# The attention gate moved from the residual to the output projection's weights, on GpSimd

## The chip, the core and the metric

The kernel runs on one core of one Trainium2 chip. The metric is the device time of one execution in microseconds. Several runs of the same kernel are given by their median.

## The reference

A decoder trunk of two layers on 256 tokens of 1024 channels. Each layer is a token mixer and a mixture of experts, both modulated by a condition c:

```python
def reference(x, c, ...):
    cs = jax.nn.silu(c)
    for i in range(DEPTH):                                # 2
        mod = (cs @ ada_w[i] + ada_b[i])[:, None, :]
        sh1, sc1, g1, sh2, sc2, g2 = jnp.split(mod, 6, axis=-1)
        hm = x * (1.0 + sc1) + sh1
        if i == 0:
            y = multiscale_pool_mixer(hm, ...)            # ... @ w_out
        else:
            y = dilated_attention_mixer(hm, ...)          # mixed @ w_out
        x = layer_norm(ALPHA * x + (1.0 + g1) * y, ln1_g[i], ln1_b[i])
        hf = x * (1.0 + sc2) + sh2
        y = moe_ffn(hf, ...)                              # 64 experts, top 8, one shared
        x = layer_norm(ALPHA * x + (1.0 + g2) * y, ln2_g[i], ln2_b[i])
    return x
```

The attention has 16 heads of 64 channels in three dilation groups. Its projection matrix is 1024 x 9216, its output matrix `attn_w_out` 1024 x 1024. The gate (1 + g1) of layer 1 has 1024 values, one for each output channel: it multiplies the columns of `mixed @ attn_w_out`.

## The kernel before

The program is written by hand, engine by engine, with semaphores. Each engine runs its own list in order. SyncE's queue issues the large loads, GpSimd's the small ones.

There are four residual-and-norm stages, n = 0 to 3: behind the pooling mixer, the first experts, the attention (n = 2) and the second experts. Stage n = 2 is what the change touches. `residual(n, t, b)` on VectorE handles token tile t (128 tokens) and channel half b (512): it waits until TensorE has finished that block of y in PSUM (`y_ready`), multiplies y by the gate in place (line 1007), adds ALPHA * x into `tmp` (line 1009, scalar_tensor_tensor) and takes bn_stats (line 1011). `variance` and `deviation` finish a tile's statistics with ScalarE's square root between them (line 740). ScalarE then writes the normalised x (line 745). TensorE transposes it, ScalarE and VectorE modulate it (lines 702 and 983), and TensorE begins the shared expert (`shared_up`, line 1430) and the router. The experts' loop comes behind.

The weights of the attention come in 40 slices of 128 x 2048 f32, 1 MB each: 36 of `attn_w_in` and, as slices 36 to 39, the four of `attn_w_out` (slice q holds its rows of two 128-channel blocks, 1024 columns each). A slice passes through these steps:

- SyncE issues its load into one of four places (`load_slice`, line 569). It first waits until slice n - 4 has been used up (`w_lo`).
- ScalarE rounds it to fp32r into one of three pairs of parts (`slice_high(n)`, line 839), after the landing (`raw_in`) and after TensorE is done with slice n - 3.
- VectorE subtracts, which leaves the low part (`slice_low(n)`, line 470, `w_lo`).
- TensorE multiplies with three products for each block: high by high, low by high, high by low (lines 1589 to 1591). `project(n)` does this for slices below 36, `out_project(c)` for the output matrix. Block c = 7 is the last; it needs the last head.

ScalarE copies each projection out (line 868) and takes slice n + 3 right after it. The order of the heads is written out: in head h TensorE runs the projections that `proj_of_head(h)` lists, then perhaps a sum of modulations, the scores of head h + 1 (line 1655), the transposes of head h's probabilities (line 1679), more projections, and the product with v (line 1696). Output blocks 0 and 1 run in head 11, 2 and 3 in head 12, 4 and 5 in head 13, 6 in head 14, 7 behind head 15. VectorE, head by head: the ALiBi bias (line 1239) and maximum (line 1244) of the next head, the final modulation sum (`ada_final`, line 955 for a gate), a copy of transposed probabilities (line 1267), `slice_low` for the `before` projections, the copy of the head's output (line 1278), `mixed_low` (line 1255: the low part of the mixed heads, which `out_project` needs), `slice_low` for the others, and a `gemv`.

`gemv` is the second piece that matters here. Modulation vectors 16 to 23 are made on VectorE: a slice of 2 MB of `ada_w` is multiplied and summed with eight operations of 128 x 512 (the first on line 936, the others on line 938: scalar_tensor_tensor of the weights and the running sum, both in SBUF), four of them in each of two heads. The last one of a gemv signals `ada_acc`. TensorE then sums it over the partitions (`ada_sum`, line 1327 for a gate), and SyncE's queue loads the next `ada_w` slice into the same place. Slices 16 and 17 are the gate of layer 1's mixer, slices 22 and 23 that of its experts:

```python
def gemv_of_head(h):
    return (18 + h // 2, h % 2) if h < 10 else (ADA_SLICES - 1, h % 2) if 12 <= h < 14 else None

def sum_of_head(h):
    return (17 + h // 2 if h < 10 else 22) if h % 2 and 3 <= h <= 9 or h == 10 else None
```

```python
GEMV_LOADS = (9, 13, 19, 24, 28, 33, 39)
...
    for n in range(RAW, SLICES):
        if n in GEMV_LOADS:
            m = 17 + GEMV_LOADS.index(n)
            sp.wait_ge(ada_acc, m - 10)
            load_ada(m)
        sp.wait_ge(w_lo, n - RAW + 1)
        load_slice(n)
```

So the load of `ada_w` slice 23, and behind it that of weight slice 39, wait for the end of gemv 22 (`ada_acc` 13), whose second half stands in head 9. Head 10 on TensorE has `ada_sum(22)` ahead of the scores of head 11.

GpSimd applies the norms' gains (`gain`, lines 462 and 464) while the other engines go on with the next stage, loads the small vectors, and has nothing to do from 671 us to 942 us.

Of the kernel before, what the change touches and what calls it, by code (L numbers as in the profile page):

```python
# [22 lines left out]
ALU = mybir.AluOpType  # L23
# [3 lines left out]
P = 128  # L27
D = 1024
# [14 lines left out]
BATCHES = HEADS // HB  # L43
# [14 lines left out]
ALPHA = (2 * LAYERS) ** 0.25  # L58
# [70 lines left out]
def build(nc, a, out):  # L129
    ctx = ExitStack()  # L130
    with ctx:
        def sb(name, shape, dt=F32):
            return ctx.enter_context(nc.sbuf_tensor(name, shape, dt))

        def sem(name):
            return ctx.enter_context(nc.semaphore(name))
# [6 lines left out]
        x = sb("x", [P, TT, D])  # L143
        gate = sb("gates", [P, 2, D])
# [47 lines left out]
        def phase(name, byte, shape, dt=F32):  # L192

            return nc.alloc_sbuf_tensor_at(name, shape, dt, offset=arena + 4 * UNITS * UNIT + byte)
# [18 lines left out]
        tmp = phase("residual_or_h", 0, [P, TT, D])  # L213
# [30 lines left out]
        def units(u0, n):  # L244
            return W[:, u0 * UNIT:(u0 + n) * UNIT]
# [52 lines left out]
        RAW = 4  # L298
        RAW_UNITS = (9, 10, 5, 8)
        SLICES = 9 * BATCHES + 4  # L300

        def slice_w(n):
            return units(RAW_UNITS[n % RAW], 1).rearrange("p (k n) -> p k n", k=KD)
# [6 lines left out]
        sum_mm, sum_read, gate_in = sem("ada_sum_mm"), sem("ada_sum_read"), [sem(f"gate_bias_in{i}") for i in range(2)]  # L310
# [10 lines left out]
        y_read = sem("y_read")  # L321
# [8 lines left out]
        shw_in = sem("shared_in")  # L330
        raw_in = [sem(f"slice_in{n}") for n in range(RAW)]
        w_hi, w_lo = sem("slice_high"), sem("slice_low")
        dist_in = sem("dist_in")
        proj_mm, proj_copied = sem("proj_mm"), sem("proj_copied")
        s_mm, s_biased, max_ready, p_exp, t_mm = sem("s_mm"), sem("s_biased"), sem("max_ready"), sem("p_exp"), sem("p_T_mm")
# [67 lines left out]
        def mixer_bank(n, t):  # L403

            return ((4, 0), (0, 2), (6, 4), (0, 2))[n][t]
# [46 lines left out]
        def gain(engine, ops, step, n, tiles=range(TT)):  # L452

            engine.wait_ge(lnp_in, 32 * (n + 1))
            if n < 3:
                engine.wait_ge(hT_mm, 4 * n + 8)
            if n in (0, 2):
                engine.wait_ge(hi_ready, TT * (n // 2 + 1))
                engine.wait_ge(lo_ready, TT * (n // 2 + 1))
            for t in tiles:  # L460
                engine.wait_ge(norm_ready, TT * n + t + 1)
                step(ops.tensor_tensor(x[:, t], x[:, t], lnp[:, 0], ALU.mult))
                step.settle()
                ops.tensor_tensor(x[:, t], x[:, t], lnp[:, 1], ALU.add).then_inc(x_ready[t], 1)
            for t in tiles:
                engine.wait_ge(x_ready[t], n + 1)
# [145 lines left out]
        def _(pool):  # L612
            step = Steps(pool, pool_steps)
            G = nc.gpsimd
            def load_norm(n):
                L, s = n // 2, n % 2
                for i, name in enumerate((f"ln{s + 1}_g", f"ln{s + 1}_b")):
                    pool.dma_start(lnp[:, i, :], a[name][L][None, :].broadcast_to([P, D])).then_inc(lnp_in, 16)

            def load_router(L):  # L620
                pool.dma_start(rw[:, :, :], a["router_w"][L].rearrange("(p k) e -> p k e", k=KD)).then_inc(rw_in, 16)
# [50 lines left out]
            pool.wait_ge(proj_copied, 1)  # L672
            gain(pool, G, step, 1)
            load_norm(2)
            pool.wait_ge(o_ready, HEADS)
            load_router(1)
            first_values(1)
# [8 lines left out]
        def _(act):  # L686
# [146 lines left out]

            def slice_high(n):
                if n < SLICES:
                    act.wait_ge(raw_in[n % RAW], 16 * (n // RAW + 1))
                    if n >= 3:
                        act.wait_ge(proj_mm, n - 2)
                    copy(wr[n % 3][:, 0], slice_w(n)).then_inc(w_hi, 1)  # L839

            load_sqrt()
            ada_copy(12)
            slice_high(0)
            ada_copy(13)
            norm(1, (0,))
# [5 lines left out]
            for t in range(TT):  # L851
# [7 lines left out]
                for half in range(2):  # L859
                    ks = slice(4 * half, 4 * half + 4)  # L860
                    copy(tokens_in(hThi, ks, t), tokens_out(t, ks)).then_inc(hT_act, 1)
            slice_high(1)
            slice_high(2)

            def projected(n):
# [52 lines left out]
        def _(dve):  # L918
            step = Steps(dve, dve_steps)
            V = nc.vector  # L920
# [80 lines left out]
            def residual(n, t, b):  # L1001

                y = PS[:, mixer_bank(n, t) + b, :]
                c = slice(b * HALF, (b + 1) * HALF)
                count = 2 * TT * n + 2 * t + b + 1
                dve.wait_ge(y_ready, count)
                V.tensor_tensor(y, y, gate[:, n % 2, c], ALU.mult).then_inc(y_read, 1)
                dve.wait_ge(y_read, count)
                step(V.scalar_tensor_tensor(tmp[:, t, c], x[:, t, c], ALPHA, y, ALU.mult, ALU.add))
                step.settle()  # L1010
                step(V.bn_stats(stats[:, t, b], tmp[:, t, c]))

# [754 lines left out]
```

## Time and profile before

| | us |
|---|---|
| median of 3 runs | 1489.09 (1487.87 to 1489.23) |
| the profiled execution | 1488.59 |
| its span | 1486.4 |
| busy: TensorE | 1425.0 (96%) |
| busy: VectorE | 577.5 (39%) |
| busy: ScalarE | 407.9 (27%) |
| busy: GpSimd | 57.7 (4%) |

The span has these stages: the pooling layer and its router to about 185 us, the first experts' loop to 630, the attention from 630 to 943, norm, shared expert and router of layer 1 to 991, the second experts' loop to the last norm at about 1475. The TensorE weight load overlaps its matmuls. A line of the timeline gives start, duration, engine, source line, operation, tiles, and in brackets how long the engine sat idle before it and who ended that. Where several instructions are merged, the duration is that of the group and xN the count. A line of busy time by stretch gives the stretch and its length in us, then busy us and (x instructions) of TensorE's matmuls, its weight loads, VectorE, ScalarE and GpSimd, the granted clock, the DMA engines' mean busy share and GB/s. The granted clock is that of TensorE as a share of 2.4 GHz: 1.00 or 0.50.

### The profile page before, as it was taken

The page shows a single profiled execution, that of the slowest core. Times are in us where ns is not written, and L with a number is a line of the kernel's source. Part 1 is how long each engine was busy: PE and PEld are TensorE (multiplying, and loading weights), DVE is VectorE, ACT ScalarE, POOL GpSimd, SP SyncE. Part 2 cuts the span into 40 slices and gives each one's busy share as a digit, 9 for nine tenths or more (in the row PEclk, how much of TensorE's full clock was granted, in tenths as well). Part 3 has the DMA queues.
Part 4 walks back from the last instruction along what each step waited for, and adds up shares of the span by engine and source line. Part 5 has one row for each costly group of instructions (what it writes and reads, how often), then busy time and mean ns, then how long its engine had stood idle before and what let it go on. Part 6 is the DMA issues. An engine that isn't in the chain of part 4 may idle for free.

```text
span 1486.4 us, 19346 instructions
## 1 busy us (share of the span) xinstructions
PE 1425.0 (96%) x7546; PEld 809.1 (54%) x7546; DVE 577.5 (39%) x1109; ACT 407.9 (27%) x636; POOL 57.7 (4%) x44
## 2 busy tenths in 40 slices
PE   6999999999999999989999999699999999999994
PEld 3544444444444444479999998454444444444442
DVE  0575122222222222377767668642222222222225
ACT  1223121212121212254555445421111111212122
POOL 0001300000000000030000000002000000000001
PEclk9999999999999999989999999899999999999997
DMA  9995899999999999968356451659999999999990
GB/s 391 423 427 216 328 413 426 426 427 424 429 424 428 424 428 425 425 263 340 118 195 251 183 203 45 255 213 416 426 427 425 428 425 427 425 427 426 425 397 28
DMA packets 50511, 522.16 MB, mean 351 GB/s; under 512 B 5632, under 2 KB 5888, under 8 KB 8224
## 3 DMA queue, kind: packets, MB, share of 16 engines
q1 hardware_dynamic: 48512, 514.61, 83.3%
q0 software_dynamic: 1952, 6.88, 1.3%
q8 instruction: 34, 0.56, 0.1%
q14 instruction: 13, 0.11, 0.0%
HBM read 520.42 MB, written 1.05 MB: 351 GB/s over the span
## 4 chain that ended last, share of the span: by engine, by line
PE 89%; DVE 4%; DMA 4%; ACT 2%; issue 1%; SPq 0%; DVEq 0%; ACTq 0%
PE psum L1538 30%; PE psum L1563 15%; PE psum L1490 9%; PE psum L1499 9%; PE psum L1589 5%; PE psum L1590 5%; PE psum L1591 5%; DMA weights<-in_ada_w 3%; PE psum L1430 2%; PE psum L1358 2%; DMA weights<-in_sh_w_down 1%; PE psum L1550 1%; PE psum L1696 1%; PE psum L1455 1%; PE psum L1679 1%; PE psum L1403 1%
## 5 line engine op out<-in xcount | busy, mean ns | idle before, releaser
L1538 PE MATMUL psum<-weights,slots_of_tokens 128*64 128x512 f32 x2048 | 450.4, 592 | 0.0
L1538 PEld LDWEIGHTS psum<-weights,slots_of_tokens 128*64 128x64 f32 x2048 | 146.9, 137 | 292.7 <-issue 292.7
L1563 PE MATMUL psum<-weights,hidden_T 128*64 128x512 f32 x1024 | 233.8, 598 | 0.0
L1192 DVE SCALAR_TENSOR_TENSOR slot_rows<-psum,slot_weight,slot_rows 128x512 fp32r<-128x512 f32 x128 | 96.1, 751 | 193.9 <-ACT slot_rows L829 193.9
L1178 DVE TENSOR_TENSOR hidden<-gate,psum 128x256 f32<-128x256 f32 x64 | 27.0, 421 | 368.3 <-ACT gate L821 368.3
L1490 PE MATMUL psum<-slot_matrix,h_parts 128*128 128x512 f32 x576 | 157.3, 399 | 0.0
L1499 PE MATMUL psum<-slot_rows,slots_T 128*128 128x512 f32 x528 | 139.3, 406 | 3.7 <-DVE slot_rows L1192 3.7
L1563 PEld LDWEIGHTS psum<-weights,hidden_T 128*64 128x64 f32 x1024 | 67.8, 136 | 132.8 <-issue 132.8
L821 ACT ACTIVATE gate<-psum 128x256 f32<-128x256 f32 x64 | 24.6, 384 | 404.6 <-PE psum L1538 404.6
L1499 PEld LDWEIGHTS psum<-slot_rows,slots_T 128*128 128x128 f32 x528 | 94.0, 188 | 74.6 <-issue 57.3
L829 ACT ACTIVATE slot_rows<-psum,slot_weight 128x512 fp32r<-128x512 f32 x128 | 88.0, 687 | 136.3 <-PE psum L1563 136.3
L1589 PE MATMUL psum<-h_transposed_high,slice_parts 128*128 128x256 f32 x384 | 111.1, 289 | 6.2 <-DVE h_transposed_low L1222 6.2
L1490 PEld LDWEIGHTS psum<-slot_matrix,h_parts 128*128 128x128 f32 x576 | 103.6, 189 | 19.2 <-issue 1.0
L1590 PE MATMUL psum<-h_transposed_low,slice_parts 128*128 128x256 f32 x384 | 109.6, 286 | 0.0
L1591 PE MATMUL psum<-h_transposed_high,slice_parts 128*128 128x256 f32 x384 | 109.5, 285 | 0.0
L470 DVE TENSOR_TENSOR slice_parts<-weights,slice_parts 128x2048 fp32r<-128x2048 f32 x40 | 91.3, 2298 | 24.3 <-ACT slice_parts L839 24.3
L1180 DVE CAST slots_T<-psum 128x256 fp32r<-128x256 f32 x64 | 27.2, 425 | 161.2 <-PE psum L1552 161.2
L1589 PEld LDWEIGHTS psum<-h_transposed_high,slice_parts 128*128 128x128 f32 x384 | 74.7, 194 | 8.0 <-issue 7.6
L823 ACT COPY hidden_T<-psum 128x256 f32<-128x256 f32 x64 | 23.8, 373 | 190.2 <-PE psum L1552 190.2
L839 ACT CAST slice_parts<-weights 128x2048 fp32r<-128x2048 f32 x40 | 75.7, 1895 | 0.0
L1590 PEld LDWEIGHTS psum<-h_transposed_low,slice_parts 128*128 128x128 f32 x384 | 74.8, 195 | 0.0
L1591 PEld LDWEIGHTS psum<-h_transposed_high,slice_parts 128*128 128x128 f32 x384 | 74.7, 195 | 0.0
(187 smaller groups left out, 1421.2 us busy)
## 6 DMA issues: line engine op xcount, KB each, us to landing
weights<-in_exp_w_gu SPq DMA_DIRECT2D x128, 2048.0 KB, 14.4
weights<-in_exp_w_down SPq DMA_DIRECT2D x128, 1024.0 KB, 13.9
weights<-in_attn_w_in SPq DMA_DIRECT2D x36, 1024.0 KB, 5.4
weights<-in_ada_w SPq DMA_DIRECT2D x12, 2048.0 KB, 19.5
slots_of_tokens<-in_ada_w SPq DMA_DIRECT2D x11, 2048.0 KB, 8.6
weights<-in_pool_w_in SPq DMA_DIRECT2D x2, 2048.0 KB, 25.9
weights<-in_pool_w_out SPq DMA_DIRECT2D x2, 2048.0 KB, 23.3
weights<-in_sh_w_gu SPq DMA_DIRECT2D x2, 2048.0 KB, 10.4
```

Source lines behind the costliest of these rows:

```text
L470: ops.tensor_tensor(wr[n % 3][:, 1], slice_w(n), wr[n % 3][:, 0].bitcast(F32), ALU.subtract).then_inc(w_lo, 1)
L829: nc.scalar.activation(yw[:, 0, half * HALF:(half + 1) * HALF], PS[:, BD + half, :], ACT.Copy, scale=wslot[:, 0:1]).then_inc(lo.yh, 1)
L839: copy(wr[n % 3][:, 0], slice_w(n)).then_inc(w_hi, 1)
L1192: V.scalar_tensor_tensor(yw[:, 1, c], PS[:, BD + half, :], wslot[:, 0:1], yw[:, 0, c].bitcast(F32), ALU.mult, ALU.subtract).then_inc(lo.yl, 1)
L1358: last = mm(PS[:, u_bank(half, t), :], hT[:, k, t * P:(t + 1) * P], w_in[part][:, k - 4 * part, half * HALF:(half + 1) * HALF], start=k == ...
L1490: last = mm(PS[:, bank, :], hfs[:, s, t, k, :], Pm[b][:, t, :], start=s == 0 and t == 0, stop=s == 1 and t == TT - 1)
L1499: last = mm(PS[:, 2 * t + half, :], PT[:, t * P:(t + 1) * P], yw[:, s, half * HALF:(half + 1) * HALF], start=False, stop=True, skip_group_ ...
L1538: last = mm(PS[j * SLOTS:(j + 1) * SLOTS, BGU, :], XgT[ob][:, k, s0:s0 + SLOTS], gu_w(ws + j)[:, k, :], start=k == 0, stop=k == KD - 1, ti ...
L1563: last = mm(PS[j * SLOTS:(j + 1) * SLOTS, BD + half, :], HT[:, k, j * SLOTS:(j + 1) * SLOTS], dn_w(ws + j)[:, k, half * HALF:(half + 1) * ...
L1589: mm(out, *parts(0, 0), start=first, stop=False)
L1590: mm(out, *parts(1, 0), start=False, stop=False)
L1591: return mm(out, *parts(0, 1), start=False, stop=last)
```

## The change

For the attention's norm the gate no longer multiplies y. GpSimd multiplies the four slices of the output matrix by the gate in place, after their landing and before ScalarE rounds them. ScalarE waits for GpSimd (`w_gated`) where it waited for the landing. `residual` leaves the product out for n = 2; for the others it stays, and `y_read` is signalled by the scalar_tensor_tensor in place of the product.

```diff
@@ semaphores
+        w_gated = sem("slice_gated")
@@ GpSimd
             gain(pool, G, step, 1)
             load_norm(2)
+            pool.wait_ge(sum_read, 18)
+            for n in range(9 * BATCHES, SLICES):
+                pool.wait_ge(raw_in[n % RAW], 16 * (n // RAW + 1))
+                rows = slice_w(n).rearrange("p k n -> p (k n)").rearrange("p (k n) -> p k n", k=2)
+                G.tensor_tensor(rows, rows, gate[:, 0:1, :].broadcast_to([P, 2, D]), ALU.mult).then_inc(w_gated, 1)
             pool.wait_ge(o_ready, HEADS)
             load_router(1)
@@ ScalarE, slice_high(n)
-                    act.wait_ge(raw_in[n % RAW], 16 * (n // RAW + 1))
+                    if n < 9 * BATCHES:
+                        act.wait_ge(raw_in[n % RAW], 16 * (n // RAW + 1))
+                    else:
+                        act.wait_ge(w_gated, n - 9 * BATCHES + 1)
@@ VectorE, residual(n, t, b)
                 dve.wait_ge(y_ready, count)
-                V.tensor_tensor(y, y, gate[:, n % 2, c], ALU.mult).then_inc(y_read, 1)
+                if n != 2:
+                    step(V.tensor_tensor(y, y, gate[:, n % 2, c], ALU.mult))
+                    step.settle()
+                V.scalar_tensor_tensor(tmp[:, t, c], x[:, t, c], ALPHA, y, ALU.mult, ALU.add).then_inc(y_read, 1)
                 dve.wait_ge(y_read, count)
-                step(V.scalar_tensor_tensor(tmp[:, t, c], x[:, t, c], ALPHA, y, ALU.mult, ALU.add))
                 step.settle()
                 step(V.bn_stats(stats[:, t, b], tmp[:, t, c]))
```

## Rows read from the trace of the kernel before

**Rows 1.** Busy time by stretch, 100 us of the second experts' loop.
```profile
1100.00:1200.00 100.00, 100.00 (x462) 46.05 (x460) 26.12 (x53) 20.36 (x35) 0.00 (x0) 1.00 1.01 426
```

**Rows 2.** Timeline, VectorE, the attention's norm: start us, duration us, instruction.
```profile
943.65 0.70 DVE L1007 TENSOR_TENSOR psum<-psum,gates 128x512 f32<-128x512 f32 x1 [1.62 <-PE psum L1591]
944.39 0.69 DVE L1009 SCALAR_TENSOR_TENSOR residual_or_h<-x,psum 128x512 f32<-128x512 f32 x1
...
952.93 0.15 DVE L1018 TENSOR_SCALAR mean_variance<-mean_variance 128x1 f32<-128x1 f32 x1
```

**Rows 3.** Timeline, TensorE, last output product and first matmul of the shared expert.
```profile
946.35 0.40 PE L1591 MATMUL psum<-slice_parts,h_transposed_high 128*128 128x512 f32 x1
...
955.47 5.70 PE L1430 MATMUL psum<-weights,h_transposed 128*128 128x512 f32 x8 [1.58 <-ACT h_transposed L702]
```

**Rows 4.** Shared down weights: issue on SyncE's queue; DMA view, us to landing last.
```profile
942.48 0.43 SPq L511 DMA_DIRECT2D weights<-in_sh_w_down  x1
...
weights<-in_sh_w_down SPq DMA_DIRECT2D x1, 1024.0 KB, 10.3
```

**Rows 5.** Timeline, GpSimd: two products in other stages, then two beside the VectorE operations of rows 8.
```profile
129.71 0.73 POOL L648 TENSOR_TENSOR shared_hidden<-shared_hidden,shared_gate 128x256 f32<-128x256 f32 x1 [7.23 <-ACT shared_gate L764]
...
175.49 2.37 POOL L464 TENSOR_TENSOR x<-x,norm_gain_bias 128x1024 f32<-128x1024 f32 x1
...
658.75 4.34 POOL L464 TENSOR_TENSOR x<-x,norm_gain_bias 128x1024 f32<-128x1024 f32 x1
663.05 2.59 POOL L462 TENSOR_TENSOR x<-x,norm_gain_bias 128x1024 f32<-128x1024 f32 x1
```

**Rows 6.** Slices 37, 38, 39: issue, then the DMA view of that issue, us to landing.
```profile
878.44 0.33 SPq L569 DMA_DIRECT2D weights<-in_attn_w_out  x1
...
weights<-in_attn_w_out SPq DMA_DIRECT2D x1, 1024.0 KB, 4.8
...
880.65 0.33 SPq L569 DMA_DIRECT2D weights<-in_attn_w_out  x1
...
weights<-in_attn_w_out SPq DMA_DIRECT2D x1, 1024.0 KB, 5.7
...
887.10 0.43 SPq L569 DMA_DIRECT2D weights<-in_attn_w_out  x1
...
weights<-in_attn_w_out SPq DMA_DIRECT2D x1, 1024.0 KB, 10.0
```

**Rows 7.** Timeline, ScalarE: it rounds slice 37.
```profile
892.19 1.89 ACT L839 CAST slice_parts<-weights 128x2048 fp32r<-128x2048 f32 x1
```

**Rows 8.** Timeline, VectorE, beside the last two of rows 5.
```profile
660.75 2.62 DVE L936 TENSOR_SCALAR modulation_sums<-slots_of_tokens,condition_silu 128x512 f32<-128x512 f32 x1
663.41 2.77 DVE L938 SCALAR_TENSOR_TENSOR modulation_sums<-slots_of_tokens,condition_silu,modulation_sums 128x512 f32<-128x512 f32 x1
```

**Rows 9.** Timeline of head 9 and 10: VectorE's subtraction and second half of gemv 22, TensorE's sum.
```profile
881.38 2.29 DVE L470 TENSOR_TENSOR slice_parts<-weights,slice_parts 128x2048 fp32r<-128x2048 f32 x1 [0.46 <-ACT slice_parts L839]
883.59 3.11 DVE L938 SCALAR_TENSOR_TENSOR modulation_sums<-slots_of_tokens,condition_silu,modulation_sums 128x512 f32<-128x512 f32 x4
...
891.50 1.02 PE L1327 MATMUL psum<-modulation_sums,constants 128*128 128x512 f32 x2
```

**Rows 10.** Timeline, VectorE, head 10: slices 36 and 37, then the mixed heads.
```profile
897.70 4.47 DVE L470 TENSOR_TENSOR slice_parts<-weights,slice_parts 128x2048 fp32r<-128x2048 f32 x2
...
902.31 1.28 DVE L1255 TENSOR_TENSOR h_transposed_low<-mixed_heads_T,h_transposed_high 128x512 fp32r<-128x512 f32 x2
```

**Rows 11.** Timeline, TensorE, head 11; output blocks 0 and 1 between the two.
```profile
902.73 1.06 PE L1679 MATMUL psum<-constants,scores 128*128 128x128 f32 x8 [0.26 <-DVE mixed_heads_T L1278]
...
909.68 1.09 PE L1696 MATMUL psum<-probabilities_T,qkv 128*64 128x128 f32 x16 [0.42 <-DVE probabilities_T L1267]
```

**Rows 12.** Busy time by stretch, columns as in rows 1; the clock is third from the end.
```profile
40.00:80.00 40.00, 38.02 (x123) 23.11 (x122) 25.03 (x38) 11.05 (x22) 0.00 (x0) 0.96 1.01 425
...
42.00:44.00 2.00, 0.22 (x2) 0.13 (x2) 1.53 (x5) 1.51 (x4) 0.00 (x0) 1.00 1.09 455
```

## The prediction, made before the change had run

> **What bounds the kernel now.** I first asked what the later half of the span is paced by. In the expert loop TensorE is busy for the whole of each stretch while the DMA engines also run near their top rate [rows 1]. So a microsecond gained or lost before that loop moves the end by a microsecond, and nothing in the loop gives it back. The change touches two places ahead of the loop: the residual and norm behind attention (943 to 955 us), and the last four weight slices (862 to 920 us). I read the first on VectorE's and TensorE's timelines, then who waits for whom in the second.
>
> **What the change removes.** Behind attention VectorE runs, four times over, a product by the gate in PSUM (line 1007), a scalar_tensor_tensor (1009) and bn_stats (1011). The first product starts at 943.65 and the next step at 944.39, so one product is 0.74 us on VectorE's queue [rows 2]. TensorE has issued its last product at 946.35 (done 946.75) [rows 3]. With the products gone VectorE would run 943.65, 945.0, 946.8 (after the 0.4 us of variance) and 948.4 for its four blocks. TensorE's results are there before each of these, so no wait takes the products' place: the variance that ended at 952.93 + 0.15 [rows 2] would end at about 950.2. Four times 0.72 is 2.9 us gained on that variance. What TensorE waits for at 955.47 [rows 3] is ScalarE's modulated columns. They stand behind the first tile's norm, which only three of the products hold up (3 x 0.72 = 2.2 us), and behind the second tile's root, which all four do. So they come 2.2 to 2.9 us earlier. There is a second floor. The shared expert's weights also have to be there: issued at 942.48, landed 10.3 us later, at 952.8 [rows 4]. That caps the gain at 955.47 - 952.8 = 2.7. The gain is 2.2 to 2.7 us; I take 2.4.
>
> The other three norms keep their products. Their y_read now comes one instruction (0.7 us) later. Only GpSimd's gate loads wait for it, hundreds of microseconds before those gates are used: cost nothing.
>
> **What it adds.** GpSimd multiplies slices 36 to 39 (128 x 2048 f32, both inputs in SBUF) in place. Its tensor_tensor takes 0.73 us on 256 columns and 2.37 on 1024 [rows 5], so 2.135 ns a column, and 2.37 + 1024 x 0.002135 = 4.56 us for 2048. The bounds are 4.5 and 4.8 (twice 2.37 and a bit), since the row is straight and the forms differ only in the gate read twice. The Trainium skill (GPSIMD Engine Reference, section 3.1) gives 4497 ns for a two-input f32 operation of this size; by an estimate from it, the sum would be 0.2 us lower over three of them.
>
> ScalarE now waits for the gated slice, not for the landing. Slice 37 is issued at 878.44 and lands 4.8 later at 883.24; slice 38 at 880.65, landing 5.7 later at 886.35 [rows 6]. ScalarE wants slice 37 at 892.19 [rows 7], slices 38 and 39 later. Each gated slice is ready before, even with GpSimd held up as below (888.2 and 893.5). Slice 36 lands at about 867 and meets VectorE idle. GpSimd has nothing queued behind these waits but the router load, which waits for the last head anyway. So the new wait itself costs nothing, and it costs at once if a gating slips by over 4 us.
>
> **The cost that decides: GpSimd and VectorE hold each other up.** The trace of before has one stretch where both work on SBUF. GpSimd's 1024-column product at 658.75 took 4.34 instead of 2.37 while VectorE ran a subtraction. Then VectorE's tensor_scalar at 660.75 took 2.62, and its scalar_tensor_tensor at 663.41 took 2.77 [rows 5, 8], where four of the same form take 3.11 with nothing beside them, 0.78 each [rows 9]. The ends fit a strict alternation: GpSimd's first product ends at 663.09, VectorE's at 663.37, GpSimd's next at 665.64, VectorE's next at 666.18. Whoever waits goes in when the other's instruction ends, and holds the other for its whole length. By this rule each of the new operations can hold VectorE for 4.56 us.
>
> [...]
>
> First collision. GpSimd asks for slice 37 at 883.3, while VectorE subtracts (881.38 + 2.29 = 883.67). It is let in at 883.67 and holds until 888.23. VectorE's four modulation products, 3.11 us together from 883.59 [rows 9], then get one turn (to 888.98). GpSimd, with slice 38 long there, takes 888.98 to 893.54. The other three products end at 893.54 + 3 x 0.78 = 895.9, where before they ended at 886.7. TensorE needs their sum: ada_sum(22) ran at 891.50 with no wait [rows 9]. It now waits until 895.9: **+4.4 us** on TensorE, the scores of head 11 and all behind them.
>
> Second collision. The end of the same products releases SyncE's last modulation load and slice 39. Its issue at 887.10 goes to 896.3, and it landed 10.0 us after issue [rows 6], so 906.3. VectorE's subtractions 36 and 37, which ran from 897.70 for 4.47 us, now run 902.1 to 906.57 [rows 10]. GpSimd asks at 906.3 and is let in at 906.57, to 911.13. The subtraction for mixed heads (line 1255), due at 902.31 + 4.4 = 906.7, waits until 911.13: **+4.4 us** more. VectorE has no slack there: TensorE's step at 909.68 waited 0.42 for VectorE's copy [rows 10, 11]. Total +8.8 us at that point. A slice 39 that lands up to 2 us sooner or later hits the subtraction before or after, for nearly the same price. From here TensorE, ScalarE and VectorE hand over to each other head by head, so the delay carries to the end.
>
> Third, the clock. In this trace TensorE was busy 0.22 of 2.00 us at 42 to 44 at a granted clock of 1.00, and the mean over 40 to 80 is 0.96 [rows 12]: at 0.5 (1.2 GHz) that is 40 x 0.04 / 0.5 = 3.2 us at the lower level. The new idle times (4.4 us at 891.5, some 3.5 us before 911) are longer than this one. Each fall would cost at most half of 3.2, 1.6 us. At the second, 1.2 us of it is covered, since TensorE's out-projection behind the wait takes 5.5 us (903.79 to 909.26 before [rows 11]), to 917.3, and VectorE's copy then comes at 918.5. Bounds 0 and 3.2; I take 1.0.
>
> **Sum.** -2.4 + 4.4 + 4.4 + 1.0 = +7.4 us. The profiled execution took 1488.59 (span 1486.4 and 2.2 around it), which gives 1496.0; the median of the runs, 1489.09, is 0.5 above it, so 1496.5.
>
> **The rivals.**
> - VectorE keeps its turn: its four products go ahead of GpSimd because each is queued before the former is done. Then they end at 886.7, TensorE waits for nothing, GpSimd does 37 and 38 by 895.8, and slice 39, landed at 897.1 as before, takes GpSimd 897.1 to 901.7. VectorE's subtraction at 897.70 waits 4.0 us. Time: -2.4 + 4.0 = +1.6, 1490.7, or with a clock fall 1492. Against it stand the rows at 663.41, where GpSimd got its turn between products of this very form. Chance 0.16.
> - No collision reaches the path (the side of no loss). The mechanism is that a GpSimd operation whose second input is the gate shared by both halves lets VectorE in, or that landings shift so that GpSimd works in VectorE's idle times. It decides if the modulation products end before 891.5. Price -2.4 to -2.9 (the whole 4 x 0.72): 1486.7. For it: slice 36 does fall into idle time, and VectorE rests between its last modulation product (886.7) and the scores that TensorE starts after 891.5. Against: slice 38 lands before the products could end. Chance 0.14, of which 0.05 for over 0.2% faster.
> - Worse: both clock falls at full price, and a third hold on VectorE because the shifted work meets GpSimd once more: +6.4 + 3.2 + up to 4.5, 1499 to 1503. Chance 0.10.
> - That the change does not do what it says (gating off the path but the products still run) would be the first collision without the gain; the diff skips them for the third norm, so it gets no share of its own.
>
> **How the numbers follow.** The forecast gets 0.60. A measurement of this kernel tells about 0.2% (3 us) from no change. Slower by over that: 0.60 + 0.10 = 0.70; within it: 0.16 + 0.09 = 0.25; faster: 0.05. The forecast alone spans 1494 to 1500 (clock 0 to 3.2, operation 4.5 to 4.8). For 8 in 10 the range reaches down to the rivals, 1487, which leaves out most of the no-collision case, and up to 1501.
>
> **What the profile of after would show.** Four GpSimd products of 2048 columns, three of them longer than 4.6 us or with VectorE operations beside them that take 4 us more than usual. The modulation products near 884 spread over 12 us instead of 3.1. TensorE waiting 4 us for them before ada_sum at 891.5. SyncE's slice 39 issued near 896, not 887. A VectorE subtraction at line 1255 of some 5 us. The last out-projection matmul about 8.8 to 10 us later than 946.75, and from it to the shared expert's first matmul 2.4 us less than 9.1. Wrong would be: modulation products of 0.78 throughout, a start of the third norm unshifted, or a third norm that is not shorter because a landing of the shared weights takes over.

## The result, and the profile after

The changed kernel took 1498.14 us (median of 5 runs, 1495.58 to 1501.36), the kernel before 1489.23 beside it. The ratio is 1.0061, with a 95% interval of 1.005 to 1.0072: 8.9 us slower. Of those runs the profiled one is the slowest, 1501.36 us with a span of 1499.6, so its trace shows more than the median has. The runs spread over 6 us, those of the kernel before over 3. A second profile of the same kernel, of a run of 1495.64 us stands under "The change once more".

The first hold, on the timeline of the changed kernel: GpSimd's two products (line 680), VectorE's four modulation products (line 947), TensorE's sum (line 1338).

```profile
868.40 4.58 POOL L680 TENSOR_TENSOR weights<-weights,gates 128x2048 f32<-128x2048 f32 x1 [197.54 <-DMA weights<-in_attn_w_out]
...
884.00 4.89 POOL L680 TENSOR_TENSOR weights<-weights,gates 128x2048 f32<-128x2048 f32 x1 [11.02 <-DMA weights<-in_attn_w_out]
...
888.84 5.04 POOL L680 TENSOR_TENSOR weights<-weights,gates 128x2048 f32<-128x2048 f32 x1
...
884.33 5.11 DVE L947 SCALAR_TENSOR_TENSOR modulation_sums<-slots_of_tokens,condition_silu,modulation_sums 128x512 f32<-128x512 f32 x1
...
889.47 4.96 DVE L947 SCALAR_TENSOR_TENSOR modulation_sums<-slots_of_tokens,condition_silu,modulation_sums 128x512 f32<-128x512 f32 x1
...
884.33 11.68 DVE L947 SCALAR_TENSOR_TENSOR modulation_sums<-slots_of_tokens,condition_silu,modulation_sums 128x512 f32<-128x512 f32 x4
...
896.06 2.08 PE L1338 MATMUL psum<-modulation_sums,constants 128*128 128x512 f32 x2 [3.67 <-DVE modulation_sums L947]
```

Alone, the product takes 4.58. The two engines then take turns: GpSimd to 888.9, VectorE's first product to 889.4, GpSimd to 893.9, VectorE's second to 894.4, and the last two without company. The four products that took 3.11 in [rows 9] take 11.68. A held instruction is not shown idle. It is shown long, with a start time from before its turn. TensorE waits 3.67 us for their sum, where it had waited for nothing [rows 9].

The second hold: SyncE's issue of slice 39, the DMA view of that issue (last column: us to landing), GpSimd's product, VectorE's subtractions 36 and 37 (line 471), and TensorE in head 11.

```profile
896.40 0.43 SPq L570 DMA_DIRECT2D weights<-in_attn_w_out  x1
...
weights<-in_attn_w_out SPq DMA_DIRECT2D x1, 1024.0 KB, 9.9
...
906.37 4.56 POOL L680 TENSOR_TENSOR weights<-weights,gates 128x2048 f32<-128x2048 f32 x1 [12.49 <-DMA weights<-in_attn_w_out]
...
904.25 8.84 DVE L471 TENSOR_TENSOR slice_parts<-weights,slice_parts 128x2048 fp32r<-128x2048 f32 x2
...
913.63 1.94 PE L1690 MATMUL psum<-constants,scores 128*128 128x128 f32 x8 [3.69 <-DVE mixed_heads_T L1289]
...
922.71 1.09 PE L1707 MATMUL psum<-probabilities_T,qkv 128*64 128x128 f32 x16
```

The issue has gone from 887.10 [rows 6] to 896.40. The landing at 906.3 falls among VectorE's subtractions, and the pair that took 4.47 [rows 10] takes 8.84. TensorE waits 3.69 us in head 11.

Busy time by stretch around the two waits (stretch, length, busy us and instructions of TensorE, its weight loads, VectorE, ScalarE, GpSimd, then the granted clock, the DMA share and GB/s):

```profile
892.00:894.00 2.00, 0.39 (x4) 0.19 (x2) 2.00 (x1) 1.57 (x2) 1.88 (x1) 1.00 0.00 0
894.00:896.00 2.00, 0.00 (x0) 0.00 (x0) 1.93 (x3) 0.81 (x1) 0.00 (x0) 0.80 0.00 0
896.00:898.00 2.00, 1.94 (x2) 0.50 (x2) 0.01 (x1) 0.00 (x0) 0.00 (x0) 0.50 0.67 131
...
910.00:912.00 2.00, 0.00 (x0) 0.00 (x0) 2.00 (x1) 1.30 (x1) 0.93 (x1) 1.00 0.00 0
912.00:914.00 2.00, 0.36 (x2) 0.40 (x3) 2.00 (x4) 0.00 (x0) 0.00 (x0) 0.57 0.00 0
```

In both waits TensorE's clock falls to 0.50 (1.2 GHz), and stays there for 6.8 us by the stretches that follow. The kernel before stood at 1.00 from 884 to 942. It was at 0.50 for 13.7 us around its norm (942 to 960), where this trace has 17.0 (952 to 974).

The norm, and what follows it: VectorE's first and last step, then the shared down weights' issue and time to landing, then TensorE.

```profile
957.74 0.69 DVE L1019 SCALAR_TENSOR_TENSOR residual_or_h<-x,psum 128x512 f32<-128x512 f32 x1 [1.90 <-PE psum L1602]
...
964.09 0.15 DVE L1029 TENSOR_SCALAR mean_variance<-mean_variance 128x1 f32<-128x1 f32 x1
...
956.28 0.43 SPq L512 DMA_DIRECT2D weights<-in_sh_w_down  x1
...
weights<-in_sh_w_down SPq DMA_DIRECT2D x1, 1024.0 KB, 11.2
...
967.57 6.72 PE L1441 MATMUL psum<-weights,h_transposed 128*128 128x512 f32 x8 [1.79 <-DMA weights<-in_sh_w_down]
```

The norm takes 964.09 - 957.74 = 6.35 us, before 952.93 - 943.65 = 9.28 [rows 2]: 2.93 less. TensorE's first matmul then waits for a transfer, where it had waited for ScalarE [rows 3]. The following table goes through this trace beside that of before, by the start of the same step:

| step | before | after | later by | what was added |
|---|---|---|---|---|
| VectorE, subtraction 35 | 881.38 | 882.12 | 0.7 | 0.7, ahead of everything changed |
| TensorE, sum in head 10 | 891.50 | 896.06 | 4.6 | 3.8, first hold |
| VectorE, bias of head 11 | 893.64 | 900.19 | 6.6 | 2.0, clock |
| VectorE, head 10's output copied | 902.09 | 913.01 | 10.9 | 4.4, second hold |
| TensorE, product with v, head 11 | 909.68 | 922.71 | 13.0 | 2.1, clock |
| VectorE, first step of the norm | 943.65 | 957.74 | 14.1 | 1.1, clock |
| VectorE, second variance | 952.93 | 964.09 | 11.2 | -2.9, the products |
| TensorE, shared expert | 955.47 | 967.57 | 12.1 | 0.9, landing |
| TensorE, second tile's transposes | 961.01 | 974.13 | 13.1 | 1.0, clock |
| span | 1486.4 | 1499.6 | 13.2 | nothing in the loop |

### The profile page after: what moved, and what is told of

It is laid out like the page before. It is cut to its first block, busy times and chain, and to the rows that moved or that the text cites. A ratio compares the mean times of both kernels' runs of the same rounds, so it can differ in the third digit from the quotient of the medians.

```text
span 1499.6 us, 19363 instructions
## 1 busy us (share of the span) xinstructions
PE 1435.8 (96%) x7546; PEld 816.4 (54%) x7546; DVE 588.0 (39%) x1105; ACT 408.0 (27%) x636; POOL 76.7 (5%) x48
## 4 chain that ended last, share of the span: by engine, by line
PE 91%; DVE 4%; DMA 3%; ACT 1%; issue 1%; SPq 0%; DVEq 0%; ACTq 0%
PE psum L1549 29%; PE psum L1574 15%; PE psum L1501 9%; PE psum L1510 9%; PE psum L1600 5%; PE psum L1601 4%; PE psum L1602 4%; PE psum L1369 2%; PE psum L1441 2%; PE psum L1414 2%; DMA weights<-in_sh_w_down 2%; PE psum L1690 1%; PE psum L1561 1%; DMA weights<-in_ada_w 1%; PE psum L1466 1%; PE psum L1707 1%
## 5 line engine op out<-in xcount | busy, mean ns | idle before, releaser
L471 DVE TENSOR_TENSOR slice_parts<-weights,slice_parts 128x2048 fp32r<-128x2048 f32 x40 | 95.7, 2407 | 23.8 <-ACT slice_parts L848 23.8
```

The source lines that it names most:

```text
L471: ops.tensor_tensor(wr[n % 3][:, 1], slice_w(n), wr[n % 3][:, 0].bitcast(F32), ALU.subtract).then_inc(w_lo, 1)
```

## The experiments

Each kernel is compared with the kernel before on the same chip. Times over or under before are the ratio less 1, times 1489. Intervals are of 95%.

### The gain alone

From the changed kernel: GpSimd's loop and ScalarE's wait for it are taken out.

```diff
-            pool.wait_ge(sum_read, 18)
-            for n in range(9 * BATCHES, SLICES):
...
-                G.tensor_tensor(rows, rows, gate[:, 0:1, :].broadcast_to([P, 2, D]), ALU.mult).then_inc(w_gated, 1)
...
-                        act.wait_ge(w_gated, n - 9 * BATCHES + 1)
+                    act.wait_ge(raw_in[n % RAW], 16 * (n // RAW + 1))
```

> The third norm leaves its four gate products out and GpSimd does nothing either: the gate of layer 1's mixer is left out of the computation. This is the gain alone. My theory (the products are on the path, and the landing of the shared weights and ScalarE cap what arrives): the second tile's variance 2.9 us earlier than before, the shared expert's first matmul 2.0 to 2.7 us earlier, time 1.5 to 2.7 us under before (ratio 0.9982 to 0.9990). Rival (the gain is eaten wholly by the landing of the shared down weights, 952.8 in before): variance 2.9 earlier, but under 1 us at the end. Rival (the products' cost was larger than read): over 3 us.

1487.47 us; ratio 0.9992 (0.9983 to 1.0001). That is 1.2 us under before, 2.5 under to 0.1 over. The timeline:

```profile
943.43 0.69 DVE L1011 SCALAR_TENSOR_TENSOR residual_or_h<-x,psum 128x512 f32<-128x512 f32 x1 [1.21 <-PE psum L1594]
...
949.77 0.15 DVE L1021 TENSOR_SCALAR mean_variance<-mean_variance 128x1 f32<-128x1 f32 x1
...
953.52 5.35 PE L1433 MATMUL psum<-weights,h_transposed 128*128 128x512 f32 x8 [2.45 <-DMA weights<-in_sh_w_down]
```

The norm is 2.9 us shorter, as in the changed kernel, but TensorE starts only 1.95 us earlier than at 955.47 [rows 3]: it waits 2.45 us, the last of it for the shared down weights. So the landing holds the gain to about 2 us on this profile, and the runs give 1.2, with an interval from nothing to 2.5.

### The loss alone

From the changed kernel: the third norm keeps its products too.

```diff
-                if n != 2:
+                if True:
                     step(V.tensor_tensor(y, y, gate[:, n % 2, c], ALU.mult))
```

> GpSimd gates the four slices as in the change and the third norm keeps its products as well, so the gate is applied twice: the loss alone. My theory (GpSimd holds VectorE twice, 4.6 us each, and TensorE's clock falls behind both stalls): modulation products near 884 take 12 us for four, and the time is 10 to 13 us over before (ratio about 1.0075), since the changed kernel was 8.9 over with a gain of 2 in it. Rival (the loss of the changed kernel comes from the norm's new order of instructions): within 2 us of before.

1497.53 us; ratio 1.0061 (1.0046 to 1.0077), 9.1 over. This is less than the 10 to 13 expected, and the same as the changed kernel. The modulation products took 11.70 us together and TensorE waited 3.68; line 1255's subtraction (1266 now) took 5.25 in place of 1.28 [rows 10], and TensorE waited 2.99 for it. The rival, that the norm's new order of instructions costs, is out: the norm keeps its products here and the loss is still there, and the run of the gain alone has the new order and no loss. The expectation was the changed kernel's 8.9 with a gain of 2 added. With intervals of some 2 us to each side, the two runs can't tell a gain of 2 from none. In this profile the clock fell behind the first stall only (the mean over 912 to 924 is 1.00, against 0.72 in the changed kernel's first profile), which is one reason for less than expected.

### The same products, placed

From the changed kernel: two more waits ahead of GpSimd's products.

```diff
             for n in range(9 * BATCHES, SLICES):
+                if n == 9 * BATCHES + 1:
+                    pool.wait_ge(ada_acc, 13)
+                if n == SLICES - 1:
+                    pool.wait_ge(w_lo, SLICES - 1)
                 pool.wait_ge(raw_in[n % RAW], 16 * (n // RAW + 1))
```

> The change with two more waits on GpSimd: slices 37 and 38 are gated only after the last modulation product of head 9, slice 39 only after VectorE's subtraction of slice 38, so each product falls where VectorE reads PSUM or rests. All of the computation is done. My theory (the whole loss is the two mutual holds and what follows from them): no VectorE operation is held, TensorE's sum at 891.5 waits for nothing, and the time is that of the kernel without any gate, 1.5 to 2.7 us under before (ratio 0.998 to 0.999). Rival (GpSimd's work costs also where VectorE reads only one tensor from SBUF): the bias and maximum steps near 894 and 906 get longer by up to 4 us each and the time is 2 to 6 us over before. Rival (slice 37 is gated too late for ScalarE at 892.2): up to 1 us given back.

1487.52 us; ratio 0.9989 (0.998 to 0.9998), 1.6 under, with the whole computation. It is as quick as the kernel without any gate. GpSimd and VectorE on the timeline:

```profile
886.26 9.15 POOL L684 TENSOR_TENSOR weights<-weights,gates 128x2048 f32<-128x2048 f32 x2 [14.61 <-DVE modulation_sums L951]
905.73 4.59 POOL L684 TENSOR_TENSOR weights<-weights,gates 128x2048 f32<-128x2048 f32 x1 [10.31 <-DVE slice_parts L471]
...
893.12 1.55 DVE L1254 SCALAR_TENSOR_TENSOR psum<-distances,psum 128x256 f32<-128x256 f32 x6 [6.94 <-PE psum L1670]
...
905.56 1.54 DVE L1254 SCALAR_TENSOR_TENSOR psum<-distances,psum 128x256 f32<-128x256 f32 x6
907.14 1.29 DVE L1259 TENSOR_REDUCE negative_maximum<-psum 128x1 f32<-128x512 f32 x2
```

GpSimd's last product (905.73 to 910.32) lies over VectorE's bias (distances from SBUF, scores from PSUM) and maximum. Neither is longer than elsewhere, and the product takes its 4.59. So an operation with one tensor in SBUF and one in PSUM is not held. The Trainium skill (SBUF — State Buffer, Who interferes with whom) states this exemption for operations with at most one SBUF input, outside what it calls the 2-port perf modes, which it says tensor_scalar can enter; this run agrees. The trace of before has both sides of it: VectorE's scalar_tensor_tensor of one tensor from PSUM and one from SBUF beside GpSimd's product, and the tensor_scalar of [rows 8] where it runs without GpSimd.

```profile
177.82 2.36 POOL L462 TENSOR_TENSOR x<-x,norm_gain_bias 128x1024 f32<-128x1024 f32 x1
179.02 0.75 DVE L1192 SCALAR_TENSOR_TENSOR slot_rows<-psum,slot_weight,slot_rows 128x512 fp32r<-128x512 f32 x1 [2.06 <-ACT slot_rows L829]
...
916.41 0.49 DVE L936 TENSOR_SCALAR modulation_sums<-slots_of_tokens,condition_silu 128x512 f32<-128x512 f32 x1
```

The first pair is not held, 2.36 and 0.75. The tensor_scalar reads a single tensor, from SBUF, and yet its 0.49 became 2.62 behind GpSimd's product [rows 8]. So one SBUF tensor alone does not make a VectorE operation safe.

### Half the length

From the changed kernel: GpSimd multiplies half of the columns.

```diff
-                G.tensor_tensor(rows, rows, gate[:, 0:1, :].broadcast_to([P, 2, D]), ALU.mult).then_inc(w_gated, 1)
+                G.tensor_tensor(rows[:, :, 0:HALF], rows[:, :, 0:HALF], gate[:, 0:1, 0:HALF].broadcast_to([P, 2, HALF]), ALU.mult).then_inc(w_gated, 1)
```

> The change with GpSimd's products on half of the columns of each slice (the other half of the output channels is left without a gate): 2.4 us in place of 4.6. My theory (the hold lasts one GpSimd instruction each time, and the first has 4.8 us of cover before TensorE needs the sum): four modulation products take 3.1 + 2 x 2.4 = 7.9 us and end at 891.5, so TensorE does not wait; the second hold costs up to 2.2 us; time between 2.5 under and 1 us over before. Rival (the loss goes with GpSimd's busy time, so half of the work is half of the loss): 4 to 5 us over before less half the gain, some 3 to 4 over.

1488.2 us; ratio 0.9997 (0.9987 to 1.0006), 0.4 under. Half of the work is not half of the loss: of 10.7 us over the placed version 1.2 are left (1.0061 and 0.9997 over 0.9989).

```profile
883.86 5.59 POOL L680 TENSOR_TENSOR weights<-weights,gates 128x1024 f32<-128x1024 f32 x2 [13.21 <-DMA weights<-in_attn_w_out]
...
884.29 7.28 DVE L947 SCALAR_TENSOR_TENSOR modulation_sums<-slots_of_tokens,condition_silu,modulation_sums 128x512 f32<-128x512 f32 x4
...
892.20 1.02 PE L1338 MATMUL psum<-modulation_sums,constants 128*128 128x512 f32 x2
...
903.01 3.25 DVE L1266 TENSOR_TENSOR h_transposed_low<-mixed_heads_T,h_transposed_high 128x512 fp32r<-128x512 f32 x2
```

The products end at 891.57, and TensorE comes to them without a wait at 892.20. Between 886.7 and 891.5 VectorE has 4.8 us that nobody waits for. Two holds of 2.4 go into it, two of 4.6 do not. The second hold is there, 3.25 in place of 1.28 [rows 10], about as long as what the shorter norm gives back.

### One hold at a time

Each of the two added waits of the placed version, alone: first without the hold on the modulation products, then without the one on the subtractions.

> The change with one more wait: GpSimd gates slices 37 and 38 only after the last modulation product of head 9; slice 39 still right after its landing. Only the first hold is taken away. My theory (two holds, each with its own price): the modulation products take 3.1 us and TensorE's sum waits for nothing; SyncE issues slice 39 near 887 again, it lands near 897, ahead of VectorE's subtractions of slices 36 and 37 (from 897.7), and GpSimd holds one of them for about 4 us; time 1.5 to 4 us over before. Rival (the second hold exists only because the first one has shifted the landing): no hold, time as with the placed products, 1 us under before.

1492.8 us; ratio 1.0024 (1.0014 to 1.0033), 3.6 over. The modulation products took 3.11 again, slice 39 was issued at 886.93, and

```profile
896.86 4.60 POOL L682 TENSOR_TENSOR weights<-weights,gates 128x2048 f32<-128x2048 f32 x1 [1.09 <-DMA weights<-in_attn_w_out]
...
897.54 8.28 DVE L471 TENSOR_TENSOR slice_parts<-weights,slice_parts 128x2048 fp32r<-128x2048 f32 x2
```

the subtractions 36 and 37 are held for 3.8 us. So the second hold does not need the first.

> The change with one more wait: GpSimd gates slice 39 only after VectorE's subtraction of slice 38; slices 37 and 38 right after their landing as in the change. Only the second hold is taken away. My theory: four modulation products take near 12 us, TensorE waits 3.7 us for them and its clock falls once for 6.8 us, which costs up to 1.7 more; no VectorE operation of head 10 or 11 is held; with about 1 us of gain, time 3.5 to 6 us over before. Together with the run without the first hold the two losses should add up to about the 9 us of the run with both. Rival (the holds hide each other: one alone costs as much as both): 8 to 9 us over.

1492.99 us; ratio 1.0027 (1.0017 to 1.0037), 4.0 over. The modulation products took 11.68, the subtractions their 4.47. Against the placed version (0.9989) the one hold costs 0.0035, the other 0.0038, together 0.0073 or 10.9 us. The changed kernel stands 0.0072 above the placed version, and 0.0066 in its second set of runs. The ratios are known to about 0.001 each; within that the two prices add up. Each price has the clock in it: both profiles have 0.50 for 6.8 us behind the one wait.

### GpSimd that only writes

From the changed kernel: three fills in place of the product, so the output projection's weights are a constant.

```diff
-                G.tensor_tensor(rows, rows, gate[:, 0:1, :].broadcast_to([P, 2, D]), ALU.mult).then_inc(w_gated, 1)
+                for part in range(2):
+                    step(G.memset(slice_w(n), 0.01))
+                    step.settle()
+                G.memset(slice_w(n), 0.01).then_inc(w_gated, 1)
```

> GpSimd fills each of the four slices three times with a constant in place of gating them, 3 x 1.8 = 5.4 us a slice, so it works as long as before and writes SBUF but reads nothing. The output projection is left out in effect: its weights are a constant. My theory (what the two engines share here is the reading of a second operand from SBUF): VectorE's four modulation products take 3.1 us, no operation is held, and the time is 0 to 2 us under before, or up to 1 over if the longer work makes ScalarE wait for slice 37. Rival (any GpSimd work on SBUF holds VectorE): the products take 3.1 plus several times 1.8 us and the time is 4 to 9 us over before.

1486.96 us; ratio 0.9985 (0.9976 to 0.9994), 2.2 under. GpSimd's fills from 883.74 to 887.4 lie over VectorE's modulation products:

```profile
883.74 3.68 POOL L680 MEMSET weights<- 128x2048 f32 x2 [10.17 <-DMA weights<-in_attn_w_out]
887.48 1.82 POOL L682 MEMSET weights<- 128x2048 f32 x1
...
884.13 3.11 DVE L949 SCALAR_TENSOR_TENSOR modulation_sums<-slots_of_tokens,condition_silu,modulation_sums 128x512 f32<-128x512 f32 x4
```

Neither engine is held, and VectorE's two subtractions at 898.25 (4.47 us) lie under the fills of slice 39 in the same way. So the hold needs GpSimd to read: its reads stand against VectorE's operations with two SBUF tensors, and against the tensor_scalar of [rows 8]. Whether a fill would hold that tensor_scalar no run shows.

### The clock behind the first stall

The version without the second hold, and TensorE works while it waits:

```diff
                 n = sum_of_head(h)
+                if n == 22:
+                    pe.wait_ge(sum_read, 22)
+                    for k in range(32):
+                        mm(PS[:, 5, 0:T], hThi[:, k % 8, 0:P], hThi[:, k % 8, :], start=True, stop=True)
                 if n is not None:
                     ada_sum(n)
```

> The change without the second hold, and TensorE runs 32 matmuls of 256 columns (3.8 us) into a bank that the next sum overwrites, right ahead of the sum for which it waits 3.7 us. The stall stays as long; only TensorE's idleness in it is gone. All of the computation is done. My theory (part of the first hold's price is the clock, 0.50 for 6.8 us behind the stall): the granted clock stays 1.00 from 892 to 904, the modulation products still take near 12 us, and the time is 1.5 to 2.5 us below that of the run without the second hold, so 1 to 2.5 us over before. Rival (the clock costs nothing, as VectorE is what the heads wait for): as without the filling, 3.5 to 4 us over before.

1490.84 us; ratio 1.0014 (1.0005 to 1.0023), 2.1 over, against 4.0 without the filling. Busy time from 892 to 904, first without, then with the filling:

```profile
892.00:896.00 4.00, 0.75 (x1) 0.50 (x2) 3.12 (x3) 2.01 (x2) 1.07 (x1) 0.79 0.00 0
896.00:904.00 8.00, 8.00 (x47) 6.35 (x46) 4.59 (x12) 2.38 (x6) 0.00 (x0) 0.68 0.97 374
```

```profile
892.00:896.00 4.00, 4.00 (x28) 3.14 (x29) 2.35 (x3) 1.20 (x1) 0.30 (x1) 1.00 0.24 49
896.00:904.00 8.00, 8.00 (x80) 7.72 (x78) 7.24 (x13) 3.87 (x9) 0.00 (x0) 1.00 0.89 366
```

The stall is as long (the products took 11.73), the clock stays up, and some 1.9 us come back. The two intervals overlap a little, 1.0017 to 1.0023, so the size is less sure than the clock's row. The two profiles also differ at the norm, 13.7 us at 0.50 without the filling and 10.2 with it, so not all of the difference need be the stall's. Against the placed version the first hold costs 5.7 us (1.0027 over 0.9989), of which 3.7 are left with the stall filled (1.0014) and 1.9 are the clock.

### The landing of the shared weights

The placed version, and SyncE loads the shared gate and up weights as soon as the slices are used up, near 924. Then the same early load in the kernel before.

```diff
             sp.wait_ge(w_lo, SLICES)
-            sp.wait_ge(o_ready, HEADS)
             shared(1)
...
                 sp.dma_start(gu_w(3), a["sh_w_gu"][L].rearrange("(p k) n -> p k n", k=KD)).then_inc(shw_in, 16)
+                if L == 1:
+                    sp.wait_ge(o_ready, HEADS)
                 sp.dma_start(dn_w(3), ...
```

> The placed products of the earlier run, and SyncE issues the shared expert's gate and up weights (2 MB) as soon as all slices are used up, near 924, and not behind the last head; the down weights (1 MB) still behind the last head. All of the computation is done. My theory (of the 2.9 us taken off the norm about 1 is lost to the landing of the shared weights): the down weights land 5 to 6 us after their issue in place of 10.5, TensorE's first matmul of the shared expert waits for ScalarE and not for a DMA, and the time is 1.5 to 3 us under before, up to 1 us under the placed run. Rival (the rest of the gain goes to TensorE's clock, which is low there either way): as the placed run, 1.0 under before.

1486.59 us; ratio 0.9984 (0.9974 to 0.9993), 2.4 under: the best version here. The down weights' time to landing, and TensorE's first matmul of the shared expert:

```profile
weights<-in_sh_w_down SPq DMA_DIRECT2D x1, 1024.0 KB, 4.8
...
953.12 6.63 PE L1446 MATMUL psum<-weights,h_transposed 128*128 128x512 f32 x8 [1.58 <-ACT h_transposed L713]
```

TensorE waits for ScalarE again. That the earlier load makes the placed version quicker is not shown: the 0.7 us between the two lie within the intervals, and in the placed version's own profile TensorE's wait there (1.58 us, at 955.23) was for VectorE, as the clock had fallen from 930 on and the norm had come late. The eight matmuls take 6.63 us, 5.70 in [rows 3]; by their length more of them ran at the lower clock.

> The kernel before, with nothing but the earlier load of the shared expert's gate and up weights (near 924). My theory (in the kernel before the shared weights land at 952.8, ahead of TensorE's need at 955.5, so this load costs something only once the norm is shorter): the same time as before, within 0.5 us. Rival (the load behind the last head also slows the expert loads right after it, or the loop's first experts): 1 us or more under before, and then the gain of the placed products with the early load is the load's, not the gate's.

1488.55 us; ratio 1.0001 (0.9992 to 1.001). The early load alone is worth nothing within 1.5 us: in the kernel before the landing is covered.

### The change once more

> The changed kernel once more, for a second profile of it and for its time beside the others of this chip. My theory: 7 to 11 us over before again; the two holds at the same places; what differs between its runs is how often and how long TensorE's clock stands at 0.50 between 892 and 975 us (30 us in all in the first profile, the slowest of its runs). Rival (the spread comes from where the slices land): the holds move by microseconds and with them the time.

1495.99 us (1495.64 to 1499.83); ratio 1.0055 (1.004 to 1.0071), 8.2 over. This profile is of a run of 1495.64 us. The first hold is the same (11.68). The second fell one operation later, on line 1255's subtraction (1266 now):

```profile
905.67 6.39 POOL L680 TENSOR_TENSOR weights<-weights,gates 128x2048 f32<-128x2048 f32 x1 [12.45 <-DMA weights<-in_attn_w_out]
...
907.82 5.39 DVE L1266 TENSOR_TENSOR h_transposed_low<-mixed_heads_T,h_transposed_high 128x512 fp32r<-128x512 f32 x2
```

and the clock stood at 0.50 for less time: 3.4 us behind each of the two waits in place of 6.8, and 6.8 around the norm. That is 13.7 us from 884 to 976, against 30.6 in the first profile and 13.7 in the kernel before (each stretch's length times twice its shortfall from 1.00). The same steps as in the table above, by how much later than in the kernel before:

| what was added | first profile | second profile |
|---|---|---|
| ahead of everything changed | 0.7 | 0.1 |
| first hold | 3.8 | 3.8 |
| second hold | 4.4 | 4.1 |
| the products gone | -2.9 | -2.9 |
| landing | 0.9 | 0.8 |
| clock, all steps named so | 6.2 | 1.6 |
| span | 13.2 | 7.5 |

The two spans differ by 5.7 us, and 4.6 of it is in the steps named clock. These are what is left of a step when the others are taken off; that it is the clock is read from the clock column, not measured apart, except behind the first stall. The record has the mean granted clock of every run too: of the nine runs of this kernel the three quickest (1495.58 to 1495.73 us) have 0.984, the slowest (1501.36) 0.977. So the spread goes with the clock. Why it stays down for longer in some executions is open.

## Why the prediction was right, and where it was off

The forecast was 1496.5 and slower. Measured were 1498.14 and, the second time, 1495.99. The mechanism was the one that the prediction put first. That the sum came so near is in part luck: the two holds were put too high (8.8; 8.2 and 7.9 in the two profiles), the clock too low and the gain a little too high, and these errors offset each other.

- **What bounds the kernel.** Right. The delay of 13.1 us at 974 is 13.2 at the end of the span, and in the second profile 7.4 at 968 is 7.5 at the end.
- **The alternation.** Right. Read from four operations [rows 5, 8], it gave 12.3 us for the four modulation products (883.59 to 895.9); they took 11.68. GpSimd's product was put at 4.56 and took 4.58. The difference is mostly in VectorE's turns: I gave the first held product 0.75, and it needed 0.55 (888.89 to 889.44). The prediction took the stretch around 660 us for the only one where both engines work on SBUF. There are others, the pair at 177.82 and 179.02 among them, which would have shown beforehand an operation that is not held.
- **The first hold.** Put at 4.4, it was 3.8 in the table, by the shorter turns, and, with its clock, 0.0038 of the time or 5.7 us against the placed version.
- **The second hold.** Right in its size (4.4; 4.1 in the second profile) and its cause, the issue of slice 39 at 896.3 (896.40) and its landing at 906.3. The operation named, line 1255, was the one held in the second profile. In the first, slowed by the clock, it was the subtraction of slice 37, for nearly the same price, as the prediction allowed.
- **The new wait of ScalarE.** Right: it rounded slice 37 at 892.92, 0.7 later than in [rows 7] like everything else there.
- **The clock.** Mis-sized in the first profile. It was put at 1.0, with 3.2 us at the lower level for each fall. The level lasted 3.4 us behind each wait in the second profile, near what the prediction worked out, and 6.8 in the first. The steps lengthened by it sum to 1.6 and 6.2 us. Filling the first stall gave back 1.9. The claim that 1.2 us of the second fall is covered failed in the first profile: TensorE's product with v at 922.71 no longer waits for VectorE, since the out-projection itself had become late. What the prediction left out is the norm, where the clock was at 0.50 for 13.7 us before, 17.0 and 6.8 after.
- **The gain.** Somewhat too high. The 2.9 us of the norm came (2.93 in both profiles). The floor by the landing was read and named, but with 2.7 as its price, from one landing of 10.3 us. It was the floor in both profiles of the changed kernel, with landings of 11.2 and 10.3 us, and in the run of the gain alone, with 10.7; TensorE gained 2.0, 2.2 and 1.95. The time gained was 1.2 us (0 to 2.5) in the run of the gain alone, which does not exclude the 2.4.
- **Where the first set of runs came out above.** By the table it is the clock, 6.2 us where 1.0 was put. The second set came out 0.5 below the forecast, and its profile has 1.6.
- **The signs named.** The last out-projection matmul was to come 8.8 to 10 us later: it came 14.1 later in the first profile and 8.5 in the second. From it to the shared expert's first matmul was to be 2.4 us less: it was 2.0 and 1.0 less.
- **The rivals.** That VectorE keeps its turn is out by the rows of the first hold. That no hold reaches the path is out for this change, but it describes the placed version: the same GpSimd work, with each product where VectorE rests or reads PSUM, is 1.6 us quicker than before.

## What to carry to other kernels

Work moved to GpSimd is not free because GpSimd is idle: each of its reading instructions can stop VectorE for its whole length. Where VectorE had 4.8 us to spare, two holds of 2.4 us made nobody wait and two of 4.6 made TensorE wait 3.7 us; whether the same work cut into more, shorter instructions would be cheaper was not tried. Look at which VectorE operations with two SBUF tensors (or a tensor_scalar that reads SBUF) lie in its window, and which of them another engine waits for; a wait on their semaphore ahead of the GpSimd instruction moves it out of their way. A stage that gets shorter meets the next transfer behind it, so look at that load too.

## What the runs showed of the hardware that was not expected

- A GpSimd fill (1.8 us for 2048 columns) lies over VectorE's products without holding either engine, where a GpSimd product of the same columns holds it for 4.6. The same page and section of the Trainium skill says so of GpSimd instructions that only write; the run agrees.
- A stall of 3.7 us on TensorE cost about half as much again through the clock: 0.50 for 3.4 or 6.8 us behind it, in two executions of the same kernel. Useless matmuls in the stall kept the clock at 1.00, and the kernel was some 1.9 us quicker.
- A VectorE tensor_scalar that reads one tensor, from SBUF, was held by a GpSimd product (0.49 us alone, 2.62 beside it), while operations with one tensor in SBUF and one in PSUM were not.
- 1 MB issued right behind 2 MB landed 9.9 to 11.2 us after its issue, and 4.8 with nothing ahead of it.
